# Two narrow gate slabs multiplied in two passes instead of three, the low parts of the weights in unused columns of the high parts' block

## What is computed

```python
h = rmsnorm(x, ln1[i])
hq, hk, hv, hr, ha, hatt, hgate = _split_cols(h @ w_in[i], SPLIT_SIZES)   # ha: 16 columns
log_a = jax.nn.log_sigmoid((ha @ w_a2[i] + b_a[i]).astype(jnp.float32)) / GLA_TAU
...
h = rmsnorm_2(x, pre_g)
u = h @ w_in.astype(jnp.float32)
qa, ka, va, oa, za, ia, fa, qb, kb, vb, zb = split_cols(u, EVEN_SPLITS)   # ia, fa: 4 columns each
ig = ia + b_i.astype(jnp.float32)
lf = jax.nn.log_sigmoid(fa + b_f.astype(jnp.float32))
```

## Time and profile before

| what | value |
|---|---|
| median of 3 runs | 1957.12 us (1957.0 to 1957.18) |
| the profiled execution | 1956.87 us |
| its span | 1955.2 us |
| TensorE (PE) busy | 1938.3 us, 99% |
| DVE, ACT, POOL busy | 751.9, 790.2, 854.3 us |
| granted clock of TensorE | 0.999 of full |

### The profile page before, as it was taken

The page is one execution under the profiler, slowest core; times in us unless marked ns, Lnnn a source line. Parts: engine busy times, 40 slices in busy tenths (PEclk is TensorE's granted clock), DMA queues, the critical chain, the costliest instruction groups (busy, mean ns, idle before and its releaser), DMA issues.

```text
span 1955.2 us, 25501 instructions
## 1 busy us (share of the span) xinstructions
PE 1938.3 (99%) x9216; PEld 1614.9 (83%) x9216; DVE 751.9 (38%) x1181; ACT 790.2 (40%) x1541; POOL 854.3 (44%) x654
## 2 busy tenths in 40 slices
PE   8999999999999999999999999999999999999998
PEld 6887888998888888888888888888888888888887
DVE  4411422330234322222327964212376646015652
ACT  5422444423424433333355543253456545333332
POOL 5522444524355355444343543344343454444552
PEclk9999999999999999999999999999999999999999
DMA  6333333323233333333232332233222242333331
GB/s 188 92 81 92 86 87 87 96 56 97 66 111 109 103 101 107 99 97 97 80 97 69 105 87 65 61 96 92 65 76 65 81 129 69 110 87 96 97 108 54
DMA packets 98957, 178.01 MB, mean 91 GB/s; under 512 B 10764, under 2 KB 16504, under 8 KB 98862
## 3 DMA queue, kind: packets, MB, share of 16 engines
q1 hardware_dynamic: 94148, 169.89, 29.9%
q10 hardware_dynamic: 4714, 6.82, 1.1%
HBM read 172.74 MB, written 3.93 MB: 90 GB/s over the span
## 4 chain that ended last, share of the span: by engine, by line
PE 91%; issue 4%; DVE 3%; ACT 1%; POOL 1%; DMA 0%; ACTq 0%; DVEq 0%; POOLq 0%
PE proj L1990 26%; PE proj L1992 26%; PE proj L1991 26%; POOL w_lo L599 1%; PE work L1990 1%; PE work L1991 1%; PE work L1992 1%; PE work L2502 1%; PE work L2483 1%; PE work L2218 1%; PE work L2234 1%; PE work L2085 1%; ACT arena L930 1%; PE proj L2457 1%; PE work L2121 1%
## 5 line engine op out<-in xcount | busy, mean ns | idle before, releaser
L599 POOL TENSOR_TENSOR w_lo<-w_raw,w_hi 128x512 fp32r<-128x512 f32 x632 | 848.8, 1361 | 1073.5 <-ACT w_hi L624 933.7
L1990 PE MATMUL proj<-act_hi,w_hi 128*128 128x512 f32 (+1 forms) x1312 | 495.9, 378 | 0.8 <-ACT arena L930 0.4
L624 ACT CAST w_hi<-w_raw 128x512 fp32r<-128x512 f32 x536 | 313.3, 619 | 446.1 <-PE proj L1992 423.2
L1992 PE MATMUL proj<-act_hi,w_lo 128*128 128x512 f32 (+1 forms) x1312 | 490.4, 374 | 0.0
L1991 PE MATMUL proj<-act_lo,w_hi 128*128 128x512 f32 (+1 forms) x1312 | 490.3, 374 | 0.0
L1990 PE MATMUL proj<-w_hi,act_hi 128*128 128x512 f32 x768 | 308.3, 401 | 1.3 <-DVE act_lo L1331 0.8
L1992 PE MATMUL proj<-w_hi,act_lo 128*128 128x512 f32 x768 | 300.1, 391 | 0.0
L1991 PE MATMUL proj<-w_lo,act_hi 128*128 128x512 f32 x768 | 299.7, 390 | 0.0
L1990 PEld LDWEIGHTS proj<-act_hi,w_hi 128*128 128x128 f32 x1312 | 247.1, 188 | 46.6 <-ACT arena L930 1.7
L1992 PEld LDWEIGHTS proj<-act_hi,w_lo 128*128 128x128 f32 x1312 | 247.0, 188 | 44.1
L1991 PEld LDWEIGHTS proj<-act_lo,w_hi 128*128 128x128 f32 x1312 | 247.2, 188 | 43.5 <-issue 0.5
(11 more groups left out here) (345 smaller groups left out, 1918.4 us busy)
## 6 DMA issues: line engine op xcount, KB each, us to landing
w_raw<-in_w_in SPq DMA_DIRECT2D x154, 256.0 KB, 2.8
w_raw<-in_w_in_ab SPq DMA_DIRECT2D x146, 256.0 KB, 2.7
w_raw<-in_w_mlp SPq DMA_DIRECT2D x128, 256.0 KB, 2.8
w_raw<-in_w_in_c SPq DMA_DIRECT2D x64, 256.0 KB, 2.7
w_raw<-in_w_out_ab SPq DMA_DIRECT2D x32, 256.0 KB, 2.8
w_raw<-in_w_out_c SPq DMA_DIRECT2D x32, 256.0 KB, 2.8
w_raw<-in_w_o_gla SPq DMA_DIRECT2D x16, 256.0 KB, 2.9
w_raw<-in_w_out SPq DMA_DIRECT2D x16, 256.0 KB, 2.7
```

Source lines behind the costliest of these rows:

```text
L599: return pool.tensor_tensor(w_lo[:, slot, :], w_raw[:, slot, :], w_hi[:, slot, :].bitcast(F32), ALU.subtract)
L624: act.copy(w_hi[:, b % RING, :], w_raw[:, b % RING, :]).then_inc(hi_ready, 1)
L1990: pe.matmul(out_, a_hi, b_hi, start=first, stop=False)
L1992: return pe.matmul(out_, a_lo, b_hi, start=False, stop=last)
```

## The change

Each narrow block's `w_hi` has unused columns. DVE now copies the block's low parts into them: columns 32 to 47 (`gla_a`) or 32 to 39 (`lstm_if`) of each row tile. One pass of `w_hi` against `act_hi` and one against `act_lo` then give both hi and lo products, in rows 0 on and rows 32 on of the bank: 16 matmuls where there were 24. TensorE waits for `narrow_ready`, which DVE counts, instead of `lo_ready`. The two groups of rows are added afterwards: for `gla_a` by a third place in the stack (112 rows), for `lstm_if` by a copy and an addition on DVE. The products now include lo x lo, which were left out before.

```diff
--- before.py
+++ after.py
@@ -308,7 +308,7 @@
         gla_state = view(16384, 2, GLA_HEADS, GLA_DV)
         reset, w_a2 = view(18432, SEQ), view(18944, SEQ)
         gla_att = view(18432, 4, SEQ)
-        STACK = 2 * LO_AT + GLA_RANK
+        STACK = 3 * LO_AT + GLA_RANK
         w_a2_parts, gla_a_parts = [nc.alloc_sbuf_tensor_at(name, [STACK, SEQ], F32R, offset=arena_at + 4 * at)
                                    for name, at in (("w_a2_parts", 3072), ("gla_a_parts", 3584))]
         bias = [view(20480, 4, KEYS[0]), view(21504, 4, KEYS[1]), view(22016, 4, KEYS[2])]
@@ -397,6 +397,7 @@
         ple_loaded, ple_done = sem("ple_loaded"), sem("ple_done")
         ln2_row_loaded, gate_scale_ready = sem("ln2_row_loaded"), sem("gate_scale_ready")
         r_diag_ready, r_row_full, even_gain_ready = sem("r_diag_ready"), sem("r_row_full"), sem("even_gain_ready")
+        narrow_ready = sem("narrow_ready")
         lstm_if_copied, lstm_f_moved = sem("lstm_if_copied"), sem("lstm_f_moved")
         lstm_f_ready, lstm_l1 = sem("lstm_f_ready"), sem("lstm_l1")
         lstm_rows, lstm_exps = sem("lstm_rows"), sem("lstm_exps")
@@ -436,6 +437,7 @@
         def tile(m):
             return slice(m, m + 1)
 
+        NARROW_AT = {"gla_a": 0, "lstm_if": 2}
         SUMS2_AT = {"pre0": 0, "pre1": 1}
         XN_AT = counted([("ln1", 8), ("ln2", 8), ("pre0", 8), ("pre1", 8)])
 
@@ -1297,6 +1299,14 @@
                         vec.scalar_tensor_tensor(lo, v, cols[:, gain + k:gain + k + 1], hi.bitcast(F32),
                                                  ALU.mult, ALU.subtract).then_inc(sem_, 1)
 
+            def narrow_stacked(name, width):
+                s = by_name[name][0]
+                for j in range(s.n):
+                    vec.wait_ge(lo_ready, s.first + j + 1)
+                    slot = (s.first + j) % RING
+                    hi, lo = (w[:, slot, :].rearrange("p (k c) -> p k c", c=P) for w in (w_hi, w_lo))
+                    vec.tensor_copy(hi[:, :, LO_AT:LO_AT + width], lo[:, :, 0:width].bitcast(F32)).then_inc(narrow_ready, 1)
+
             def head_scales(n):
                 vec.wait_ge(head_root_ready, n)
                 step(vec.reciprocal(rstd[:], root[:]))
@@ -1356,23 +1366,26 @@
             vec.tensor_copy(rel_rep[0:REL_BUCKETS + 1, :].rearrange("b (c r) -> b c r", r=REPS),
                             rel_rows[0:REL_BUCKETS + 1, :].unsqueeze(2).to_broadcast([REL_BUCKETS + 1, 3 * ATT_HEADS, REPS]))\
                .then_inc(rel_ready, 1)
+            narrow_stacked("gla_a", GLA_RANK)
             vec.wait_ge(cols_full, 1)
             vec.tensor_copy(cols[:, 0:CONV_AT], work[:, 3, 0:CONV_AT])
             vec.tensor_copy(cols[:, CONV_AT:CONV_AT + 64], work[:, 3, P:P + 64]).then_inc(cols_ready, 1)
             vec.wait_ge(cols_ready, 1)
             step(vec.memset(reset, 1.0))
             step(vec.memset(reset.rearrange("p (c t) -> p c t", t=CHUNK)[:, :, 0:1], 0.0))
-            LO, HI2 = slice(LO_AT, LO_AT + GLA_RANK), slice(2 * LO_AT, STACK)
+            LO, HI2, HI3 = (slice(i * LO_AT, i * LO_AT + GLA_RANK) for i in (1, 2, 3))
             for part in (w_a2_parts, gla_a_parts):
                 ins = vec.tensor_copy(part[:], reset[0:STACK, 0:1].to_broadcast([STACK, SEQ]))
             step(ins)
             vec.tensor_copy(w_a2_parts[LO, :], w_a2[0:GLA_RANK, :])
+            vec.tensor_copy(w_a2_parts[HI3, :], w_a2[0:GLA_RANK, :])
             step(vec.tensor_copy(w_a2_parts[0:GLA_RANK, :], w_a2[0:GLA_RANK, :]))
             step(vec.tensor_tensor(w_a2_parts[HI2, :], w_a2[0:GLA_RANK, :], w_a2_parts[0:GLA_RANK, :].bitcast(F32), ALU.subtract))
             wait_used(vec, (by_name["gla_a"][0], by_name["gla_a"][0].n - 1))
             a_ = work[0:GLA_RANK, 0, :]
             step(vec.tensor_copy(gla_a_parts[0:GLA_RANK, :], a_))
-            vec.tensor_copy(gla_a_parts[HI2, :], a_).then_inc(gla_a_copied, 1)
+            vec.tensor_copy(gla_a_parts[HI2, :], a_)
+            vec.tensor_copy(gla_a_parts[HI3, :], work[LO, 0, :]).then_inc(gla_a_copied, 1)
             vec.tensor_tensor(gla_a_parts[LO, :], a_, gla_a_parts[0:GLA_RANK, :].bitcast(F32), ALU.subtract)\
                .then_inc(gla_a_copied, 1)
             for pair in range(2):
@@ -1659,6 +1672,7 @@
                 vec.tensor_scalar(x[:, m, :], ple_pp[:, m, :], rstd[:, m:m + 1], None, ALU.mult).then_inc(x_final, 1)
             vec.wait_ge(r_row_full, 1)
             step(vec.tensor_copy(even_r_row, work[:, 0, :]))
+            narrow_stacked("lstm_if", 2 * LSTM_HEADS)
 
 
             H = LSTM_HEADS
@@ -1690,7 +1704,9 @@
             convolve(0, 1)
             s = by_name["lstm_if"][0]
             wait_used(vec, (s, s.n - 1))
-            step(vec.tensor_tensor(if_rows, work[0:2 * H, 1, :], even_r_row[0:2 * H, :], ALU.mult))
+            step(vec.tensor_copy(if_rows, work[LO_AT:LO_AT + 2 * H, 1, :]))
+            step(vec.tensor_tensor(if_rows, work[0:2 * H, 1, :], if_rows, ALU.add))
+            step(vec.tensor_tensor(if_rows, if_rows, even_r_row[0:2 * H, :], ALU.mult))
             vec.tensor_scalar(row["i"], if_rows[0:H], lstm_b[:, 0:1], None, ALU.add).then_inc(lstm_if_copied, 1)
             convolve(0, 2)
             vec.wait_ge(lstm_f_moved, 16)
@@ -2104,13 +2120,13 @@
             def narrow_slab(s, bank_):
 
                 for j in range(s.n):
-                    pe.wait_ge(lo_ready, s.first + j + 1)
+                    pe.wait_ge(narrow_ready, NARROW_AT[s.name] + j + 1)
                     slot = (s.first + j) % RING
                     for kk in range(4):
                         k = 4 * j + kk
                         f = slice(kk * P, (kk + 1) * P)
-                        ins = three(bank_, w_hi[:, slot, f], w_lo[:, slot, f], act_hi[:, k, :], act_lo[:, k, :],
-                                    k == 0, k == KD - 1)
+                        pe.matmul(bank_, w_hi[:, slot, f], act_hi[:, k, :], start=(k == 0), stop=False)
+                        ins = pe.matmul(bank_, w_hi[:, slot, f], act_lo[:, k, :], start=False, stop=(k == KD - 1))
                     ins.then_inc(block_used, 1)
 
             def turn_tile(src, k, ready_sem, base):
```

## The result

The changed kernel takes 1965.73 us (median of 5 runs, 1962.58 to 1966.63) against 1957.18 for the kernel before, run beside it: ratio 1.0041, 95% interval 1.003 to 1.0052. The medians lie 8.5 us apart, and its runs spread over 4 us where those of before spread over 0.5. The profiled execution is the fastest of the five, 1962.58 us with a span of 1960.9.

A forecast was written before the change was run, and what follows sets the result against it. PE, busy 99% of the span, was taken as the bound. Matmuls -3.64 and PE waits and restarts +8.29 gave +4.6 us: 1961.5 for the profiled execution, 1961.7 for the median; range 1959.3 to 1966.3.

The forecast's parts named there:

- Matmuls: Both narrow slabs on PE: eight fewer matmuls in each, 1.8 us saved twice, -3.6 us.
- The gates' chain: DVE chain to the gates behind the first slab: +1.56 and +0.71, PE idle 3.85 us; first slab +2.1 net.
- The second wait: PE at lstm_if's first narrow matmul waits about 4.2 us for DVE's copies (0.6); slab +2.5 net.
- The sum without the clock: Whole kernel: matmuls saved against PE waits and restarts, +4.6 us, 1961.7 us; chance 0.50.
- The clock: Rival at the two new PE waits: clock falls to 1.2 GHz; one fall 1963.8, two 1966.0; chance 0.34.
- The price of a fall: After a new PE wait: a low clock outlasting it by one to two times as long costs 1.4 to 2.9 us.
- The case with two falls: Clock falls at both new PE waits: 1966.0 us; one or two falls together have chance 0.34.
- Behind the second slab: raw_rows(1) frees lstm_k's bank at 1103.1, PE wants it at 1104.3: no wait; at upper bounds 1.2 us.
- The other side: Rival at both slabs: signals in time, needing the DVE queue ahead of 1078.05 3.5 us shorter; 1953.5; chance 0.04.

The follow-up runs named there:

- e7: e1 plus 6 useless matmuls ahead of the gla_a_copied wait, so that PE idles less there: 1958.80 us, +1.9 over the kernel before.
- e4: Changed kernel with DVE reordered: w_a2's parts and fills made before the first slab, lstm_if copies behind the first x scaling; 1957.93 us, ratio 1.0008.
- e5: Changed kernel with w_a2's parts early, the four x scalings moved to ACT, and narrow copies ahead of the even_r_row copy: 1953.83 us, ratio 0.9984.
- e3: Changed kernel plus useless matmuls, 12 ahead of the gla_a_copied wait and 14 ahead of the second narrow slab: 1961.02 us, +4.2 over before.
- e10: Changed kernel plus only the 12 useless matmuls ahead of the gla_a_copied wait, second wait left open: 1962.61 us, ratio 1.0031.
- e11: Changed kernel plus only the 14 useless matmuls ahead of the second narrow slab, gates' wait left open: 1963.53 us, ratio 1.0031.
- e1: Changed kernel with the second slab undone, only gla_a in two passes: 1960.60 us, +3.8 over before, ratio 1.002.
- e8: e4 without the DVE copy and addition for lstm_if, gate rows leaving out the product with the weights' low parts: 1957.61 us, ratio 1.0002.
- e9: Changed kernel unedited, measured again beside e10 and e11: 1965.61 us, ratio 1.0046.

## Why the prediction was right or wrong

The direction held, and 1965.7 lies in the range; the forecast itself, 1961.7 (1961.8 by its own terms), is 4 us short. By its steps:

**Matmuls.** Right: 9216 to 9200, the first slab 1.80 us shorter.

**The gates' chain.** Right in mechanism and nearly in size. The copy of w_a2 took the turn that was foreseen, 1.52; chain +2.05 for +2.27 forecast. Without the clock the first slab costs +1.9 (e7's median) for +2.1.

**The second wait.** Right: 3.90 us for "about 4.2", the two copies 0.61 for 0.6. (The 0.6 fits this place in the queue; elsewhere the same two took 1.35 and 2.51 us, in e4 and e5.) That w_lo is ready in time and that DVE's order alone sets the moment is borne out by e4, where an earlier place removes this wait.

**The sum without the clock.** +4.6 forecast, +4.2 measured (e3).

**The clock.** This is the step that failed. The price of a fall was bounded nearly rightly, 1.4 to 2.9 us: medians of 1.5 at the second slab and 2.4 at the gates (e10, e11), and 3.1 worked out from e1's profile. The chance was not: the prediction gave 0.34 to any fall and argued that the waits exceed by only 1 us the 2.9 us that the clock had held at the end of the trace. That one interval was read as a threshold that a wait must pass. It is none: the clock fell after waits of 1.8 us (e4, e8) and 2.0 us (e7), sometimes only after PE had resumed, and held through 3.5 us in the profiled run of e11. In the kernel before, the clock stood at 1.00 through a wait of 2.4 us at the start, longer than the waits of 1.8 and 2.0 that brought a fall. What decides it, no run here shows. The changed kernel's first profile has one fall, e9's has two, and each is the fastest run of its five. The case with two falls, 1966.0, was the one that came; the time lies in the range by this rival, and not by the sum.
The Trainium skill, TensorE: Matmul & The Clock Gate, section What's actually happening, ties the clock to how busy PE has been of late. The trace agrees so far as falls came at every place with a new wait of 1.8 to 3.9 us, in some or in most executions, and the length of the wait alone did not decide. Read so, the one interval of 2.9 us was no ground to give the falls the smaller chance.

**Behind the second slab.** "1.2 us of slack, so nothing" held in the changed kernel: DVE waited 2.1 us for PE ahead of raw_rows(1). But only because PE was late, by the waits, as forecast, and by the fall on top. In e4, where PE came 4.8 us earlier (1102.68 for 1107.47), DVE did not wait for PE there.

**The other side.** The rival "both signals come in time, 1953.5" named one point, the DVE queue ahead of the even_r_row copy. e4 met its condition for the slab and gave 1957.9: the same queue, longer by the copies' 1.28 us, then holds PE at the next bank. The rival's number was right (e5 1953.8), its condition too weak: DVE's whole order up to raw_rows(0), and then to raw_rows(1), must come earlier.

## What to carry to other kernels

Where TensorE is busy 99%, look at an edit by what TensorE will wait for, and find the producer's place in its queue: 1.8 us of matmuls saved cost a 3.9 us wait because the copy stood last. A saving just ahead of a step that another engine feeds is not gained unless that engine's chain gets shorter too; check the next two hand-overs. And a new wait on TensorE can have two prices, its length and the lower clock behind it (here from 1.8 us on, not in every run); matmuls of no use in the wait show the second, and pay it off.

## What the runs showed of the hardware

A fall of the clock is not tied to the wait's end: it came 0.65 us after PE had resumed (the changed kernel), 1.2 us after (e4), and within the wait (e1), and the low clock lasted 3.4, 3.4 and 6.8 us. At the low clock 512-column matmuls started 0.43 us apart.

DVE's copies of 32 elements per partition, from SBUF to SBUF, took 0.52 and 0.17 us in the changed kernel, 1.27 and 0.17 in e4, and 1.18 and 1.33 in e5, with POOL at work without a pause beside all three. One of 512 elements took 1.52 beside POOL and 0.42 without it. So beside a busy POOL a small copy can cost as much as a large one, but does not always; where it stands in the queue changed its price by 1 us.
